# Modulation vectors of a two-block network: from matrix products on TensorE to dot products on VectorE, as a third stream of the plan

## The chip, the cores and the metric

One core of one Trainium2 chip runs the whole program. The metric is device time in microseconds (us), from three runs of the kernel before: 3962.25, 3965.93 (the median) and 3976.16. Names as in the profile: PE is TensorE (PEld its weight loads), DVE is VectorE, ACT is ScalarE, POOL is GpSimd, SP is SyncE, which only issues transfers.

## The reference, cut to what matters

A first block (two layers of a retention and state-space mixer and a feed-forward network) acts on `x`, 256 tokens of 1024 channels. A second block (two layers) mixes tokens and routes each token to 128 experts (PEER), for `x` and, in its first layer only, for a context `ctx` of 256 tokens. All is float32. Only the second block uses the modulation:

```python
def _modulation(cvec, w_mod, b_mod):
    m = jax.nn.silu(cvec) @ w_mod + b_mod          # [1,1024] @ [1024,6144]
    return jnp.split(m[:, None, :], 6, axis=-1)
def _modulate(x, g, shift, scale):
    return _rmsnorm(x, g) * (1 + scale) + shift
...
for l in range(2):
    m_x = _modulation(c, w_mod[l], b_mod[l])
    m_c = _modulation(c_ctx[None, :], w_mod[l], b_mod[l])
    h  = _modulate(x,   norm1_g[l], m_x[0], m_x[1])
    hc = _modulate(ctx, norm1_g[l], m_c[0], m_c[1])
    ...                                            # token mixing of hc and h
    x = x + m_x[2] * mix_x
    x = x + m_x[5] * _peer(_modulate(x, norm2_g[l], m_x[3], m_x[4]), ...)
    if l == 0:                                     # the same for ctx with m_c[2..5]
```

The context's mixing needs sixths 0 and 1 of `m_c` of layer 0 at first, and the others later. In layer 1 the context needs sixths 0 and 1 alone. The vectors for `x` aren't needed before the first block has ended.

## The kernel before

One Python class, `Plan`, writes one list of items in order (`put`), and each engine's program goes through the list and issues its part of each item. So the order of items is the order of instructions on every engine, and an engine that waits holds back all that stands behind it on that engine.

Two streams feed the list. Stream `a` is `x`: the first block, then the second. Stream `b` is the context: modulation, then its mixing (`mix_phase`), then its routing and experts (`peer_c`). `streams` (L228) takes the next piece of `b` whenever b's count of time has fallen behind `pace` times a's; each piece yields a count that is meant to be microseconds of its work. The paces are the table `PACES`, one for each stage. When the first block ends, what is left of `b` is put down at once. The counts of stream `a` are the same in both kernels, so they name a place in the program below: "count 257" is 257 counted microseconds into the first block. In the kernel before, modulation stands up to count 218, the context's mixing from there to 368, its routing to 477, and its 512 gathers with their products from 477 to 1699.

Modulation (L743): the weights of both layers come as 48 tiles of 1 MB (128 input channels by 2048 outputs), issued by POOL into a ring of seven slots (the semaphores wm0 to wm6), with up to four loaded ahead. For each, PE makes four products of 128x2 (both condition vectors) by 128x512 at four column positions of the array (L1905). After eight tiles DVE adds the bias, SP stores the rows to DRAM (`mod_store`), and PE and DVE turn them into columns (`mod_columns`, with four transposes at L1691).

The first block on PE is groups of 16 products of 128x128 by 128x256 at L1656, L1836 and L1843, on pairs of PSUM banks. A group's result is taken out by ACT or DVE before its bank is used again. The groups wait there on DVE: for the convolution (`conv_end`), for turning (L2200, L2308) and for the branch products (L2345). A head's routing on DVE (`rank_keys`, `rank_pairs`, `rank_index`) is a chain of small instructions. `peer_c` gathers rows on POOL (L2980), 0.5 MB each, and takes a dot product over 1024 channels with each (L2635, function `down`) or adds it (L2646, `up`), both on DVE. A weight tile of the first block goes over SP's queue into one of three slots.

A `Slot` is a piece of SBUF with a semaphore, a `Ring` a list of slots taken in turn; a load waits until the slot's last reader is done. `rstd` on POOL is L2967.

## Time and profile before

| | |
|---|---|
| median of three runs | 3965.93 us (3962.25 to 3976.16) |
| the profiled execution: its span, first to last instruction | 3961.4 us |
| lowest run, nearest to the profiled execution; outside its span | 3962.25 us; 0.85 us |
| PE busy | 3596.4 us, 91% |
| DVE busy | 2300.7 us, 58% |
| POOL busy | 1284.5 us, 32% |
| moved from HBM | 1201.64 MB read |

The profile doesn't give a time of its own for the profiled execution beside the span. The first and last instruction are the span's ends, and the lowest run is 0.85 us above it, so the span stands for that execution's time. In the tables below, busy time is the time in which an engine worked; a busy share near 100% on PE with little on the others means that PE is what the stage waits for. A matrix product in float32 leaves two records.

### The profile page before, as it was taken

The page shows a single profiled execution, that of the slowest core. Times are in us where ns is not written, and L with a number is a line of the kernel's source. Part 1 is how long each engine was busy: PE and PEld are TensorE (multiplying, and loading weights), DVE is VectorE, ACT ScalarE, POOL GpSimd, SP SyncE. Part 2 cuts the span into 40 slices and gives each one's busy share as a digit, 9 for nine tenths or more (in the row PEclk, how much of TensorE's full clock was granted, in tenths as well). Part 3 has the DMA queues.
Part 4 walks back from the last instruction along what each step waited for, and adds up shares of the span by engine and source line. Part 5 has one row for each costly group of instructions (what it writes and reads, how often), then busy time and mean ns, then how long its engine had stood idle before and what let it go on. Part 6 is the DMA issues. An engine that isn't in the chain of part 4 may idle for free. (4 is left out here: it accounts for less than half of the span.)

```text
span 3961.4 us, 41101 instructions
## 1 busy us (share of the span) xinstructions
PE 3596.4 (91%) x14600; PEld 2547.8 (64%) x14600; DVE 2300.7 (58%) x5460; ACT 664.2 (17%) x1814; POOL 1284.5 (32%) x1130
## 2 busy tenths in 40 slices
PE   8998999989999999999999989788779998877777
PEld 6667788878876888888847876333335786433333
DVE  3342013566877887765762147777763226777775
ACT  2232101110001330000002212111112211111111
POOL 1100000023445456774650013444341003444442
PEclk9999999999999999999999999899899999998999
DMA  8752345357998889998983259999996339999997
GB/s 331 291 202 89 128 149 191 128 207 291 345 354 343 292 296 412 406 400 343 414 353 132 102 221 411 398 414 407 411 419 274 108 126 375 405 419 419 420 419 327
DMA packets 206842, 1205.50 MB, mean 304 GB/s; under 512 B 23472, under 2 KB 24640, under 8 KB 95024
## 3 DMA queue, kind: packets, MB, share of 16 engines
q0 software_dynamic: 154976, 858.34, 54.0%
q1 hardware_dynamic: 51664, 344.55, 23.0%
q8 instruction: 118, 1.93, 0.2%
q14 instruction: 84, 0.69, 0.0%
HBM read 1201.64 MB, written 1.15 MB: 304 GB/s over the span
## 5 line engine op out<-in xcount | busy, mean ns | idle before, releaser
L1656 PE MATMUL bank<-big 128*128 128x256 f32 (+4 forms) x8888 | 1909.3, 374 | 47.3 <-DVE big L2435 13.8
L1656 PEld LDWEIGHTS bank<-big 128*128 128x128 f32 (+2 forms) x8888 | 1628.9, 190 | 338.3 <-issue 90.8
L2980 POOL DMA_INDIRECT big<-in_pboth,big x1024 | 1213.2, 1185 | 1301.0 <-PE bank L2134 703.7
L2134 PE MATMUL bank<-big 128*128 128x512 f32 x2048 | 990.6, 641 | 224.7 <-ACT big L2943 224.6
L2635 DVE CUSTOM_DVE_ANT_0 big<-big 128x1024 f32<-128x1024 f32 x768 | 926.1, 1223 | 338.6 <-DMA big<-in_pboth,big 333.2
L2134 PEld LDWEIGHTS bank<-big 128*128 128x128 f32 x2048 | 409.6, 204 | 785.8 <-issue 483.8
L2646 DVE SCALAR_TENSOR_TENSOR big<-big 128x1024 f32<-128x1024 f32 x254 | 326.1, 1284 | 75.7 <-DMA big<-in_pboth,big 55.3
L2967 POOL TENSOR_TENSOR big<-big 128x1 f32<-128x1 f32 (+1 forms) x49 | 42.4, 865 | 914.5 <-DVE big L2192 914.3
L2943 ACT ACTIVATE big<-big 128x128 f32<-128x128 f32 x512 | 165.4, 391 | 270.5 <-DVE big L2612 266.0
L2933 ACT ACTIVATE big<-big 128x4 f32<-128x4 f32 (+2 forms) x136 | 28.1, 207 | 730.9 <-DVE big L2608 725.6
L1836 PE MATMUL bank<-big 128*128 128x256 f32 x576 | 129.5, 378 | 0.0
L1691 PE MATMUL bank<-big 128*128 128x128 f32 x628 | 95.3, 284 | 32.8 <-ACT big L2721 17.2
L1836 PEld LDWEIGHTS bank<-big 128*128 128x128 f32 x576 | 108.7, 189 | 15.8
L1865 PE MATMUL bank<-big 128*128 128x512 f32 x256 | 110.6, 592 | 2.2 <-DVE big L2359 2.2
L1843 PE MATMUL bank<-big 128*128 128x256 f32 x448 | 103.0, 381 | 6.0 <-DVE big L2308 4.6
L1691 PEld LDWEIGHTS bank<-big 128*128 128x128 f32 x628 | 77.0, 150 | 47.7 <-issue 29.3
L2480 DVE TENSOR_REDUCE big<-bank 128x1 f32<-128x512 f32 (+1 forms) x48 | 28.9, 602 | 135.2 <-PE bank L2004 135.1
L2345 DVE SCALAR_TENSOR_TENSOR big<-big,bank 128x256 f32<-128x256 f32 x32 | 13.5, 422 | 154.9 <-PE bank L1843 154.8
L2991 POOL DMA_DIRECT2D big<-in_iota x1 | 0.6, 584 | 306.3 <-DVE big L2516 306.3
L2249 DVE SCALAR_TENSOR_TENSOR big<-bank,big 128x255 f32<-128x255 f32 (+1 forms) x144 | 62.7, 478 | 60.8 <-ACT big L2735 59.1
L1843 PEld LDWEIGHTS bank<-big 128*128 128x128 f32 x448 | 84.7, 190 | 19.3 <-DVE big L2308 5.1
L2268 DVE SCALAR_TENSOR_TENSOR big<-big,bank 128x512 f32<-128x512 f32 x32 | 22.0, 687 | 124.0 <-ACT big L2750 114.8
(218 smaller groups left out, 2279.7 us busy)
## 6 DMA issues: line engine op xcount, KB each, us to landing
big<-in_w SPq DMA_DIRECT2D x104, 1024.0 KB
big<-in_wmod POOLq DMA_DIRECT2D x48, 1024.0 KB, 8.9
big<-in_wgu SPq DMA_DIRECT2D x44, 1024.0 KB
big<-in_wzg SPq DMA_DIRECT2D x36, 1024.0 KB, 4.8
big<-in_wro SPq DMA_DIRECT2D x32, 1024.0 KB
big<-in_wpq SPq DMA_DIRECT2D x24, 1024.0 KB, 4.9
big<-in_wd SPq DMA_DIRECT2D x22, 1024.0 KB
big<-in_pboth,big POOLq DMA_INDIRECT x1024, 11.0
```

What stands on the lines that cost most here:

```text
L1656: last = pe.matmul(o, a, b, start=(i == 0), stop=(i == n - 1))
L1691: last = pe.transpose(o[:, i, :], b, ident)
L1836: pe.matmul(u.ap[:, 0:256], wk[:, k, :], YT[:, k, :], start=(k == 0), stop=False)
L1843: last = pe.matmul(u.ap[:, 0:256], wk[:, k, :], YT[:, k, :], start=False, stop=(k == 15))
L1865: last = pe.matmul(u.ap, act[:, 2 * i + k, tt * P:tt * P + P], wk[:, k, 512 * n:512 * n + 512], start=(i + k == 0), stop=False)
L2134: last = pe.matmul(u.ap, d.ap, row[:, 512 * i:512 * i + 512], start=(k == 0), stop=(k == 127))
L2249: i = v.scalar_tensor_tensor(c[:, m, s:256], o[:, m, 0:256 - s], conv["w"][m][:, 3 - s:4 - s], c[:, m, s:256], ALU.mult, ALU.add)
L2635: v.tensor_tensor_reduce(row, row, h, 1.0, 0.0, ALU.mult, ALU.add, out).then_inc(done[0], 1)
L2646: v.scalar_tensor_tensor(at, s.ap, by, at, ALU.mult, ALU.add).then_inc(done[0], 1)
L2943: s.activation(d.ap, p.ident, ACT.Copy, scale=by).then_inc(diag[0], 1)
L2967: g.tensor_tensor(r.sm[:, 8 + r.at:8 + r.at + r.n], r.sm[:, 4 + r.at:4 + r.at + r.n], r.sm[:, 12:13].to_broadcast([P, r.n]), ALU.pow).then ...
L2980: g.indirect_dma_start(out=s.ap, out_offset=None, in_=table, in_offset=bass.IndirectOffsetOnAxis(ap=index, axis=0)).then_inc(s.full[0], 16)
```

## The change

1. The modulation becomes a third stream `m`. It advances while its own count is below `MOD_PACE` = 0.6 times a's. The context calls it directly where it needs more.
2. Its work moves to DVE. The vector silu(c) lies as a row of 1024 on all 128 partitions. A block is 128 output channels by 1024 inputs (0.5 MB), and one dot product on DVE (`tensor_tensor_reduce`) gives one column. There are 160 blocks: for the context 48 of layer 0 and 16 of layer 1, then for `x` 48 of each layer. The weights are read once for each vector, 80 MB in place of 48.
3. The blocks' slots: one spare (wm0) from the start to the end of the context's mixing, two (wm1, wm2) in the memory of `MT` until the first layer's merging, and from there, in the memory of `fw`, one (wm3).
4. The context's mixing begins when sixths 0 and 1 are there. Before its routing the plan waits for its other sixths; after its routing, before its first gather, the plan puts down all blocks that are left.
5. The columns come straight out of the dot products. Rows for DRAM are made with one 128x48 transpose on PE, one copy on DVE and one store on SP (`mod_rows`), three times. The bias is loaded into the columns at the start.
6. `PACES` changes at three places: 0.79, 0.47 and 0.73 become 0.66, 0.41 and 0.66. One gather slot (`row_end`) is made of the vector's memory.

In the counts of stream `a`: the context's mixing stands from 30 to 183, its routing to 290, the last blocks end at 304, and the gathers stand from 304 to 1691.

```diff
 
-PACES = (0.8, 1.8, 1.5, 0.79, 0.47, 0.73, 4.0)
+PACES = (0.8, 1.8, 1.5, 0.66, 0.41, 0.66, 4.0)
+MOD_PACE = 0.6
+MOD_END = 1024
 A_SIZE = 27648
 BIG_N = 53208
 SIDE = 8300
...
+        self.mod_ring, self.mod = Ring([self.mod_spare]), self.modulation()
+        self.streams(self.x_stream(ar), self.context_stream(), self.mod, PACES[0])
...
+        live = {"a": a, "b": b, "m": m}
         while live:
             which = "b" if "b" in live and (tb <= ta * pace or "a" not in live) else "a"
+            if "m" in live and tm < ta * MOD_PACE:
+                which = "m"
             step = next(live[which], "over")
             if step == "over":
...
+                tm += step
...
+        self.tick("d_ctx", 16)
+        yield 16
+        while (0, 1, 1) not in self.sixths:
+            next(self.mod)
+            yield 2
         self.put("context_in")
         yield "pace", PACES[1]
+        ar.size -= 1024
         yield from self.mix_phase(self.pb, Ring(few), self.smallb, ar, 0, self.C, 1, False)
+        self.mod_moves([self.mod_spare], [])
+        while (0, 1, 5) not in self.sixths:
+            next(self.mod)
+            yield 2
...
+        mod_slots = [Slot(MT.rearrange("p a b -> p (a b)")[:, 1024 * i:1024 * i + 1024], self.sem(f"wm{i + 1}")) for i in range(2)]
+        mod_late = Slot(fw, self.sem("wm3"))
+        self.mod_ring.slots.extend(mod_slots)
...
                 yield "pace", PACES[4]
+                for _ in self.mod:
+                    pass
...
+            else:
+                mod_late.freed = cv.slots[cv.at % 2 - 1].freed
+                self.mod_moves(mod_slots, [mod_late])
+                put("mod_moved", ready=[w.freed for w in mod_slots])
...
+    def mod_moves(self, gone, new):
+        self.mod_ring = Ring([w for w in self.mod_ring.slots if w not in gone] + new)
+        while any(w.freed == "held" for w in gone):
+            next(self.mod)
...
-                for k in range(8):
-                    while srcs and len(coming) < 4:
-                        coming.append(self.load(wr, srcs.pop(0), 2048))
-                        put("mod_weights", w=coming[-1])
-                    w = coming.pop(0)
-                    done = tick("mod_part", 4)
-                    w.free(done)
-                    if k == 3 and late:
-                        part_end()
-                    put("mod", w=w, u=u, cc=cc, k=k, ready=(self.sem("mod_c_done"), 1) if l + part + k == 0 else None,
-                        done=done)
-                    yield 3
...
+        blocks = [(l, v, b) for v in (1, 0) for l in range(2) for b in range(16 if l and v else 48)]
+        left, coming, at, done = list(blocks), [], None, None
...
+        for l, v, b in blocks:
+            if v != at:
+                tmp, at = self.mod_room().take(), v
...
+                put("mod_c", dst=vector, tmp=tmp, src=t["crow"][v].to_broadcast([P, 1024]), before=done, loaded=tick("d_c2", 16),
+                    tanh=tick("mod_tanh"), done=ready)
+                tmp.free(ready)
+            while left and left[0][1] == v and self.mod_room():
+                l2, _, b2 = left.pop(0)
+                coming.append(self.load(self.mod_room(), t["wmod"][l2, b2], 1024))
+                put("mod_weights", w=coming[-1])
+            w, done = coming.pop(0), tick("mod_part")
+            w.free(done)
+            put("mod", w=w, vector=vector, to=sums[b // 8 % 2][:, b % 8:b % 8 + 1], done=done)
+            if b % 8 == 7:
...
+                self.cols_ok = tick("mod_columns")
...
+                put("mod_sixth", sums=sums[part % 2], ready=done, dst=self.mcols[:, j, 8 * part:8 * part + 8], gain=gain,
...
+                self.sixths.add((l, v, part))
+                if part == 5:
+                    s, u, self.mods_ok[l, v] = self.mod_room().take(), self.pb.take(), tick("d_mods", 16)
...
+                    put("mod_rows", src=self.mcols[:, j, :], u=u, ready=self.cols_ok, s=s, rows=s.ap[0:48, 0:P],
+                        dst=self.mods[l, v].rearrange("s (k p) -> (s k) p", p=P), done=self.mods_ok[l, v])
+                    s.free(self.mods_ok[l, v])
+            yield 1.25
...
+        while (l, vec) not in self.mods_ok:
+            next(self.mod)
+        put("load_row", dst=m2, src=self.mods[l, vec, 2:3, :].to_broadcast([P, 1024]), done=m2_ok,
+            before=[got["aT"], got["f_ok"], self.mods_ok[l, vec]])
...
         yield from route()
+        for _ in self.mod:
+            yield 2
...
-    def mod(w, u, cc, k, ready, done):
-        if ready:
-            pe.wait_ge(*ready)
-        if k == 0:
-            opened(u)
-        pe.wait_ge(*w.full)
-        for j in range(4):
-            pe.matmul(u.ap[32 * j:32 * j + 2, :], cc[:, k, :], w.dst[:, 512 * j:512 * j + 512], start=(k == 0),
-                             stop=(k == 7), tile_position=(0, 32 * j)).then_inc(done[0], 1)
...
+        pe.transpose(u.ap[0:48, 0:P], src, ident).then_inc(u.full[0], 1)
 
...
+        v.tensor_scalar(dst, dst, 0.5, None, ALU.mult).then_inc(done[0], 1)
+        v.wait_ge(*done)
+
+    def mod(w, vector, to, done):
+        v.wait_ge(*w.full)
+        v.tensor_tensor_reduce(w.dst, w.dst, vector, 1.0, 0.0, ALU.mult, ALU.add, to).then_inc(done[0], 1)
+
+    def mod_sixth(sums, ready, dst, gain, biased, done):
+        v.wait_ge(p.sem("d_bias"), 16)
+        v.wait_ge(*ready)
+        i = v.tensor_tensor(dst, dst, sums, ALU.add)
+        if gain:
+            i.then_inc(biased[0], 1)
...
+    def mod_rows(u, rows, dst, done, **_):
...
     def mod_load(gb, sc, sh, srcs, loaded, before):
         for ok in before:
@@ -3050,7 +3073,8 @@
         q.dma_start(cs.rearrange("p a b -> p (a b)"), t["cs"]).then_inc(done[0], 16)
```

DVE at the start of the program, before (L2377 and L2379 make silu(c), L2192 is the variance, L2200 takes the turned rows out of PSUM for the first product):

```order
L2407 MEMSET big 128x512
L2377 SCALAR_TENSOR_TENSOR big<-big 128x16 [waits mod_tanh,vector_step]
L2379 TENSOR_SCALAR big<-big 128x16 [waits vector_step]
L2192 TENSOR_SCALAR big<-big 128x1 [waits squares_done] x2
L2200 TENSOR_TENSOR big<-bank,big 128x4x128 [waits full4]
L2200 TENSOR_TENSOR big<-bank,big 128x4x128 [waits full5]
L2200 TENSOR_TENSOR big<-bank,big 128x4x128 [waits full4]
```

and now (L2403, L2405: silu(c) as rows; L2410: a block's dot product and, as its second row, the read of its sum; L2226 is L2200 of before):

```order
L2218 TENSOR_SCALAR big<-big 128x1 [waits squares_done]
L2403 SCALAR_TENSOR_TENSOR big<-big 128x1024 [waits mod_tanh]
L2405 TENSOR_SCALAR big<-big 128x1024 [waits vector_step]
L2410 ISA big<-big 128x1024 [waits wm1,mod_vector]
L2410 ISA big 128x1
L2410 ISA big<-big 128x1024 [waits wm2]
L2410 ISA big 128x1
L2410 ISA big<-big 128x1024 [waits wm0]
L2410 ISA big 128x1
L2226 TENSOR_TENSOR big<-bank,big 128x4x128 [waits full4]
L2226 TENSOR_TENSOR big<-bank,big 128x4x128 [waits full5]
L2410 ISA big<-big 128x1024 [waits wm1]
```

Three blocks now stand ahead of the first take-out and a fourth between the two halves.

PE around the small product for the time steps (128x32), before, where the modulation's first products stand (L1905), and below it now, where the context's first transposes and products stand (L1727 and L1692, bank pair 6 and 7):

```order
L1656 MATMUL bank<-big 128x256 x15
L1656 MATMUL bank<-big 128x32 [waits wa1,free5,free0]
L1656 MATMUL bank<-big 128x32 x15
L1905 MATMUL bank<-big 2x512 [waits wm0,mod_c_done]
L1905 MATMUL bank<-big 2x512 x3
L1905 MATMUL bank<-big 2x512 [waits wm1]
L1905 MATMUL bank<-big 2x512 x3
L1656 MATMUL bank<-big 128x256 [waits wa2,free1]
L1656 MATMUL bank<-big 128x256 x7
```

```order
L1692 MATMUL bank<-big 128x256 x7
L1727 MATMUL bank<-big 128x128 [waits rows_scaled]
L1727 MATMUL bank<-big 128x128 x7
L1692 MATMUL bank<-big 128x256 x8
L1727 MATMUL bank<-big 128x128 [waits rows_scaled_v,free6]
L1727 MATMUL bank<-big 128x128 x3
L1727 MATMUL bank<-big 128x128 [waits free7]
L1727 MATMUL bank<-big 128x128 x3
L1692 MATMUL bank<-big 128x128 [waits free7,wb0,free6]
L1692 MATMUL bank<-big 128x128 x15
L1692 MATMUL bank<-big 32x256 [waits free7]
```

The products of two rows are gone, and the context's projection stands inside and behind the fourth group.

DVE in the first layer's merging, around the take-outs of branch products 0 and 1, before (L2308 takes out turned rows, L2345 a branch product, L2480 to L2484 the context's attention):

```order
L2484 RECIPROCAL big<-big 128x1 [waits free6]
L2308 TENSOR_TENSOR big<-bank,big 128x4x128 [waits full5]
L2308 TENSOR_TENSOR big<-bank,big 128x4x128 [waits full4]
L2345 SCALAR_TENSOR_TENSOR big<-big,bank 128x256 [waits full0,free0]
L2480 TENSOR_REDUCE big<-bank 128x1 [waits full7,free6]
L2482 TENSOR_SCALAR big<-big 128x1 [waits vector_step]
L2484 RECIPROCAL big<-big 128x1 [waits free7]
L2345 SCALAR_TENSOR_TENSOR big<-big,bank 128x256 [waits full1,free0]
L2480 TENSOR_REDUCE big<-bank 128x1 [waits full6,free7]
L2482 TENSOR_SCALAR big<-big 128x1 [waits vector_step]
```

and now, from the take-out of product 1 on (L2371), at the end of the context's routing (L2613 to L2619 its gates):

```order
L2371 SCALAR_TENSOR_TENSOR big<-big,bank 128x256 [waits full1,free0]
L2410 ISA big<-big 128x1024 [waits wm3]
L2410 ISA big 128x1
L2613 TENSOR_REDUCE big<-big 128x8 [waits vector_step,gates_exp]
L2615 TENSOR_SCALAR big<-big 128x8 [waits vector_step]
L2617 RECIPROCAL big<-big 128x8 [waits vector_step]
L2619 TENSOR_TENSOR big<-big 128x128 [waits vector_step]
L2410 ISA big<-big 128x1024 [waits wm3,gates_done]
L2410 ISA big 128x1
L2410 ISA big<-big 128x1024 [waits wm3]
L2410 ISA big 128x1
L2410 ISA big<-big 128x1024 [waits wm3]
```

Behind these rows come eleven more blocks on slot wm3 before the next take-out. Every block from the merging on waits for `wm3`: 31 of them. On PE, behind the third branch product at this place, stands the transpose of `mod_rows`, which waits for the column sums of the last of these blocks (`mod_columns`).

## Rows read from the trace of the kernel before

**Rows 1.** The page: busy time of each engine, share of the span.
```profile
PE 3596.4 (91%) x14600; PEld 2547.8 (64%) x14600; DVE 2300.7 (58%) x5460; ACT 664.2 (17%) x1814; POOL 1284.5 (32%) x1130
```

**Rows 2.** Windows by stage: length, busy us of each engine, clock, DMA share, GB/s.
```profile
0.00:263.00 263.00, 245.91 (x1434) 177.39 (x1435) 107.01 (x257) 72.66 (x189) 28.39 (x56) 1.00 0.76 296
263.00:640.00 377.00, 348.61 (x1656) 292.87 (x1655) 59.30 (x143) 62.87 (x169) 3.90 (x6) 0.96 0.34 125
640.00:800.00 160.00, 155.52 (x746) 133.45 (x745) 78.77 (x255) 22.41 (x51) 5.59 (x9) 1.00 0.43 157
800.00:2081.00 1281.00, 1237.89 (x5534) 1007.00 (x5533) 930.75 (x1677) 153.23 (x367) 672.55 (x532) 0.99 0.89 345
2081.00:3961.00 1880.00, 1608.50 (x5237) 937.08 (x5235) 1124.90 (x3130) 353.05 (x1039) 574.12 (x528) 0.94 0.81 327
```

**Rows 3.** Groups on PE by form: count of records, busy us, mean ns.
```profile
L1656 PE MATMUL bank<-big 128*128 128x256 f32 x7984 | 1772.4, 380 | 27.5 <-issue 6.6 <-DVE big L2268 5.5 <-DVE big L2200 3.6
...
L1691 PE MATMUL bank<-big 128*128 128x128 f32 x628 | 95.3, 284 | 32.8 <-ACT big L2721 17.2 <-ACT big L2769 8.5 <-DVE big L2337 4.3
L1905 PE MATMUL bank<-big 128*2 128x512 f32 x384 | 48.8, 592 | 0.0
```

**Rows 4.** Groups on DVE by form: count, busy us, mean ns.
```profile
L2635 DVE CUSTOM_DVE_ANT_0 big<-big 128x1024 f32<-128x1024 f32 x768 | 926.1, 1223 | 338.6 <-DMA big<-in_pboth,big 333.2 <-issue 3.0
...
L2635 DVE DVE_READ_ACCUMULATOR2_ANT big<- 128x1 f32 x768 | 63.3, 82 | 0.0
...
L2402 DVE TENSOR_TENSOR big<-big 128x1024 f32<-128x1024 f32 x2 | 2.5, 1226 | 0.1
```

**Rows 5.** Timeline of the start: start us, us, engine, line.
```profile
14.37 1.04 ACT L2704 ACTIVATE big<-big 128x1024 f32<-128x1024 f32 x1
...
17.70 3.96 POOL L2973 DMA_DIRECT2D big<-in_wmod  x7
...
19.34 1.29 DVE L2200 TENSOR_TENSOR big<-bank,big 128x512 f32<-128x512 f32 x2 [2.23 <-PE bank L1691]
...
22.14 31.49 PE L1656 MATMUL bank<-big 128*128 128x256 f32 x160 [0.79 <-DVE big L2200]
...
30.43 2.69 DVE L2249 SCALAR_TENSOR_TENSOR big<-bank,big 128x255 f32<-128x255 f32 x6 [8.35 <-ACT big L2735]
33.15 0.63 ACT L2743 ACTIVATE big<-big 128x512 f32<-128x512 f32 x1 [2.75 <-DVE big L2249]
33.81 0.69 DVE L2261 SCALAR_TENSOR_TENSOR big<-big 128x512 f32<-128x512 f32 x1 [0.70 <-ACT big L2743]
```

**Rows 6.** DMA issues: queue, count, KB, us from issue to landing.
```profile
big<-in_wmod POOLq DMA_DIRECT2D x48, 1024.0 KB, 8.9
...
big<-in_wout SPq DMA_DIRECT2D x12, 1024.0 KB, 4.8
...
big<-in_wukv SPq DMA_DIRECT2D x4, 512.0 KB, 3.3
```

**Rows 7.** The modulation's weight loads: issue times in ns, and time to landing.
```profile
L2973 POOL DMA_DIRECT2D big<-in_wmod x48: 527/537/760, 17.7 to 233.7; - x48
...
DMA to landing us min/median/max: 5.2/8.9/21.6
```

**Rows 8.** Timeline of DVE over most of one head's routing, first and last.
```profile
689.77 0.30 DVE L2529 MAX8 big<-big 128x8 f32<-128x128 f32 x1
...
691.62 0.42 DVE L2548 TENSOR_TENSOR big<-big 128x256 f32<-128x256 f32 x1
...
698.40 1.41 DVE L2337 SCALAR_TENSOR_TENSOR big<-bank,big 128x512 f32<-128x512 f32 x2
```

**Rows 9.** Waits over the span: who waited for whom, us, times, longest.
```profile
DVE big L2345 <- PE bank L1843: 154.8, 31, 32.8
```

**Rows 10.** Windows of 20 us in the context's mixing; columns as in Rows 2.
```profile
260.00:280.00 20.00, 13.85 (x82) 10.82 (x75) 9.91 (x26) 12.18 (x31) 1.82 (x3) 0.83 0.36 138
...
540.00:560.00 20.00, 20.00 (x94) 17.47 (x93) 3.88 (x6) 1.68 (x4) 0.00 (x0) 1.00 0.46 163
```

**Rows 11.** The context's gathers on POOL: issue times in ns, first and last start.
```profile
L2980 POOL DMA_INDIRECT big<-in_pboth,big x512: 932/1112/2055, 841.0 to 2049.9; - x171
```

196 lines of the change are left out of this document (82 added, 114 removed).

## The prediction

> **What bounds the kernel now.** I read the page's busy times first: PE is busy 91% of the span, DVE 58% [rows 1]. Then the windows by stage [rows 2]. The change acts in the first block, 0 to 2081 us. PE is busy there 245.9 + 348.6 + 155.5 + 1237.9 = 1988 of 2081 us, so nearly every microsecond taken from PE's work there is one less, and nearly every new idle one is one more. DVE has room on average: 107 + 59 + 79 + 931 = 1176 us busy. But the reader is to see in the order of DVE's instructions that it is one queue. The third view is the waits: DVE waits 154.8 us for the branch products [rows 9], so in the first layer's merging PE sets the pace and DVE stands ready. The stages behind 2081 us are not touched.
>
> **What goes from PE.** L1905 is busy 48.8 us in 384 records [rows 3], all of it in a stage where PE is nearly full. The 24 transposes that made columns are 48 records of 95.3/628 = 0.152 us each: 7.3 us. Three transposes of 48 rows come back, under 1 us. Sum: -56 us, with ends at -49 (transposes hidden in gaps) and -68 (12 us more of PE's gaps around them). I take -56.
>
> **What comes to DVE.** A block is the operation of `down`: 1.223 us, and 0.082 for the read of its sum [rows 4], so 1.305 us. 160 of them are 209 us, which on average fit in the 905 us in which DVE is idle. Each vector costs a product and a scaling besides, about 2 us, twice. So the price is not the work. It is what stands behind a block in DVE's queue while the block waits for its weights.
>
> **The round trip of a slot.** A block frees its slot, POOL issues the next load (0.53 us [rows 7]), it lands, and DVE goes on. No row has a 0.5 MB load by POOL alone. From below: the same size by SP lands in 3.3 us [rows 6]. From above: the 1 MB loads of POOL, which overlap each other, have a median of 8.9 and a least of 5.2 us [rows 7]. The 1 MB loads by SP take 4.8 [rows 6], 1.5 more than the half; 5.2 less 1.5 is 3.7, and some 0.5 us for the release and POOL's own step brings it to 4.2 us, which I take, as the nearest row is the least of POOL's. I call this e, with ends 3.3 and 8.9.
>
> [...]
>
> **Start of the program, +15.** PE's first group starts at 22.1 us, right behind the take-outs of L2200 [rows 5]. Now three blocks stand ahead of these and a fourth between them. The first load is issued when POOL has done the reciprocal roots, at about 17.7 as before [rows 5]; it lands near 21, the third near 22.5, the last take-out ends near 28. That is 6 us. In the four convolution groups DVE has 2.69 + 0.69 us of its own for each of PE's 7 us [rows 5], and now 3.4 blocks of 1.305: 7.8 us in 7, plus about 2 us whenever four blocks stand in a row for three slots (e less two blocks). PE loses some 9 us more until the context gives it other work. Ends: 5 (landings early enough) and 25.
>
> **The context's mixing, +15.** Here PE's work for both streams is the same as before, moved 190 counts earlier. DVE was busy 59 of 377 us [rows 2]; 76 blocks bring 99 us, and the first block's own share of DVE is larger at this place (107 in 263 us [rows 2]). There is room, but every take-out can find a block ahead of it, and PE was idle 28 us here by such chains already. Two places stop SP's queue as well: the store of `mod_rows` waits for DVE, and the second vector's load waits for DVE's last block of the first; the weight tile behind each is issued only then and lands 4.8 us later [rows 6], in place of two groups ahead. I take 5 us for each of them and 5 for collisions; ends 0 and 35.
>
> **The context's routing, +35.** From count 183 to 257 PE has about 105 us of work: rows 2 show 155.5 us for the same eight queries beside 109 counts of `x`; the new place to 304 has 12 counts more, so 167, less the 62 of the next part. DVE has 35 blocks (46 us), five heads of routing at 10.6 us (6.7 from the pairs to the last cast, and 2 x 1.9 for the keys [rows 8]: 53 us), about 10 for the context's rows, about 27 for `x` (0.36 of 75, the share of rows 2's first window), and since the spare slot is gone, seven times a third block waits e less one block, 2.9 us: 20. That is 156 us against 105. PE can stay ahead by its banks for a group or two, so I take 35 of the 51; ends 0 and 51.
>
> **The single slot, +121.** From the merging on all 31 blocks wait for wm3. No load can be under way while a block is computed. On DVE: 31 x 1.305 = 40.5, three heads 32, take-outs and gates 6, and the exposed round trips: 22 blocks follow another block directly (e each), four more follow something short of e (together about 3e - 2). With e = 4.2 that is 25 x 4.2 - 2 = 103. Sum 181, and with the waits for the gates' exponent 183 us. PE's work at this place, counted in its order: 128 products of 128x256 at 2 x 1772.4/7984 = 0.444 us and 16 of 128x128 at 0.30 [rows 3], 62 us. Can PE run ahead and hide it? It can't: the first branch product's end needs the turned rows, which DVE takes out behind the first 13 blocks, and then PE has 20 us of work until the transpose of `mod_rows`, which waits for the last block's sum, with 18 blocks before it. So PE waits 183 - 62 = +121 us. With e = 3.3 it is +99, with e = 8.9 +239.
>
> **Afterwards, -8.** The gathers get 1387 counts in place of 1222, so DVE and the DMA engines (0.89 full in rows 2) are less dense; PE is idle 43 us there, and I take 8 of them back; ends 0 and -20. The context still ends ahead of the first block (1691 of 1722), so there is no tail. A granted clock of 0.83, mostly the full 2.4 GHz and in part 1.2, shows where PE was idle a third of 20 us [rows 10]; PE's work behind the new waits may run so, but DVE is what ends there, so I add nothing.
>
> **Sum.** -56 + 15 + 15 + 35 + 121 - 8 = +122 us. 3961.4 + 122 = 4083 against the profiled execution's own span; the median of the runs shown lies 4.5 above it, half of which I grant: 4085 us.
>
> **Rivals.**
> 1. *The stalls don't reach PE.* Loads land as fast as DVE asks and PE's banks cover the rest: -56 - 8 and about 15 at the start and at SP's queue: 3915 us, faster than before. For it: DVE waits for PE 154.8 us at L2345 alone [rows 9], so it often has time. Against it: the transpose of `mod_rows` ties PE to DVE's last block. It decides if e is under about 1 us. Chance 0.14.
> 2. *Only the last run of blocks counts.* DVE gets far enough ahead of PE before; then 14 blocks in a row cost 14 x 5.5 - 20 = 57 in place of 121, and the routing stage nothing: 3961 - 56 + 30 + 57 - 8 = 3984 us. Chance 0.15. Against it: DVE's heads need PE's queries first.
> 3. *The round trip is as long as the median of 8.9 us.* +239 in place of +121: about 4200 us. For it: POOL's loads by rows 7. Against it: these had up to four others under way, these here have none. Chance 0.07.
> 4. *The context comes late* and leaves a tail behind the first block, since its paces are smaller: 2 to 4% of the gathers' 1280 us, 4120 us. Chance 0.03; its counts end 31 ahead.
>
> The Trainium skill ("SBUF — State Buffer", the trap in which DVE blocks DMA) says that GpSimd can't write a load's descriptors while DVE holds the shared port. By that rule a block would lengthen the next block's load, up to one block each, 1.3 x 25 = 33 us, and speak for rival 3. The 48 issues of rows 7 took 527 to 760 ns beside a DVE busy 0.4 of the time, so the trace shows none of it; and with one slot DVE stands still while the load is made.
>
> **How the numbers follow.** The forecast has 0.58, the rivals 0.14, 0.15, 0.07 and 0.03, and 0.03 is left for a time near the old one. Its own range, from e and the ends of the other terms, is 4030 to 4150. The range for all reaches down to rival 2: 3960 to 4160 holds 0.80, leaving out rival 1 and most of rival 3. Within 0.3% is 3954 to 3978, about what a measurement of this kernel can't tell from no change: 0.05, from the rest and the low edge of rival 2. Faster 0.15, slower 0.80.
>
> **What would show it.** Right: on DVE, idle time before the block's line put down to the DMA of the modulation's weights, some 100 us of it within a stretch of 180 us in which PE is busy a third; the transpose of 48 rows on PE with a wait of tens of us; PE's first group near 28 us; the first gather near 757 us in place of 841 [rows 11]: at count 304 the program has 477 - 304 = 173 us less behind it than the 800 us of count 477, 56 us less of products and 186 us more of stalls. POOL's load there every 5.5 us. Wrong: PE above 90% in every window before 700 us (rival 1), or a landing under 2 us, or the wait sitting in gathers after 700 us.

## The result, and the profile after

The changed kernel takes 4191.30 us (median of four runs, 4188.10 to 4191.73) against 3964.61 beside it: ratio 1.0572, 95% interval 1.0553 to 1.0590. The forecast was 4085 with a range from 3960 to 4160. The sign was right, but +122 us should have been +227, and the time lies outside the range.

The page's busy times after, columns as in [rows 1]:

```profile
PE 3568.5 (85%) x14195; PEld 2557.3 (61%) x14195; DVE 2477.4 (59%) x5772; ACT 664.1 (16%) x1815; POOL 1337.8 (32%) x1242
```

PE lost 28 us of work and gained 253 us of idle time. Windows by stage, as in [rows 2]: to the end of the context's mixing, its routing, the single slot up to the first gather, the rest of the first block, the second block.

```profile
0.00:532.00 532.00, 412.44 (x1945) 347.69 (x1945) 230.83 (x498) 109.21 (x285) 56.82 (x106) 0.89 0.55 199
532.00:715.00 183.00, 133.07 (x666) 114.68 (x667) 122.30 (x332) 37.82 (x102) 23.54 (x43) 0.88 0.55 196
715.00:898.00 183.00, 43.86 (x202) 37.58 (x200) 73.80 (x201) 3.96 (x8) 18.50 (x33) 0.64 0.33 103
898.00:2305.00 1407.00, 1369.17 (x6147) 1121.11 (x6147) 925.26 (x1613) 159.77 (x380) 651.61 (x533) 0.99 0.86 329
2305.00:4186.70 1881.70, 1609.92 (x5240) 936.20 (x5239) 1125.23 (x3131) 353.30 (x1041) 587.31 (x528) 0.94 0.81 327
```

The second block is as before. In the third row PE is busy a quarter of the time and DVE under half of it: both wait. Who waits there, from the groups of DVE and the waits of DVE and of PE (engine, line, for whom, us, times, longest); L2410 is a block, L1937 the transpose of `mod_rows`, L1879 the branch product's end, L2334 the take-out of turned rows:

```profile
L2410 DVE CUSTOM_DVE_ANT_0 big<-big 128x1024 f32<-128x1024 f32 x160 | 192.9, 1222 | 171.5 <-DMA big<-in_wmod 170.8
```
```profile
PE bank L1937 <- DVE big L2415: 104.6, 3, 73.1
PE bank L1879 <- DVE big L2334: 66.0, 1, 66.0
```

73.1 + 66.0 = 139.1 us is all of PE's idle time in the single-slot stage. And this is one turn of the slot on DVE and POOL (timeline: start, us, engine, line, idle time before it):

```profile
722.44 1.23 DVE L2410 CUSTOM_DVE_ANT_0 big<-big 128x1024 f32<-128x1024 f32 x1
723.59 0.08 DVE L2410 DVE_READ_ACCUMULATOR2_ANT big<- 128x1 f32 x1
723.97 0.53 POOL L2996 DMA_DIRECT2D big<-in_wmod  x1 [5.79 <-DVE big L2410]
...
727.76 1.23 DVE L2410 CUSTOM_DVE_ANT_0 big<-big 128x1024 f32<-128x1024 f32 x1 [4.08 <-DMA big<-in_wmod]
728.91 0.08 DVE L2410 DVE_READ_ACCUMULATOR2_ANT big<- 128x1 f32 x1
729.29 0.53 POOL L2996 DMA_DIRECT2D big<-in_wmod  x1 [4.79 <-DVE big L2410]
```

The block ends, POOL issues the next load 0.3 us later, DVE stands 4.08 us until it has landed. The forecast had taken 4.2. The 32 loads of this stage land 3.6 to 4.6 us after the start of their issue, 3.8 in the median, and DVE waits for 27 of them, 105.5 us in all.

### The profile page after: what moved, and what is told of

It is laid out like the page before. It is cut to its first block and busy times, and to the rows that moved or that the text cites. A ratio compares the mean times of both kernels' runs of the same rounds, so it can differ in the third digit from the quotient of the medians.

```text
span 4186.7 us, 40723 instructions
## 1 busy us (share of the span) xinstructions
PE 3568.5 (85%) x14195; PEld 2557.3 (61%) x14195; DVE 2477.4 (59%) x5772; ACT 664.1 (16%) x1815; POOL 1337.8 (32%) x1242
## 5 line engine op out<-in xcount | busy, mean ns | idle before, releaser
L1692 PE MATMUL bank<-big 128*128 128x256 f32 (+6 forms) x8888 | 1919.3, 376 | 79.6 <-DVE big L2456 21.5
L1692 PEld LDWEIGHTS bank<-big 128*128 128x128 f32 (+2 forms) x8888 | 1640.4, 191 | 352.1 <-issue 89.7
L2160 PE MATMUL bank<-big 128*128 128x512 f32 x2048 | 994.5, 643 | 222.3 <-ACT big L2966 221.2
L2656 DVE CUSTOM_DVE_ANT_0 big<-big 128x1024 f32<-128x1024 f32 x768 | 925.1, 1223 | 319.3 <-DMA big<-in_pboth,big 317.4
L2160 PEld LDWEIGHTS bank<-big 128*128 128x128 f32 x2048 | 411.3, 205 | 785.8 <-issue 490.1
L2996 POOL DMA_DIRECT2D big<-in_wmod x160 | 85.2, 533 | 700.5 <-DVE big L2410 675.7
L2990 POOL TENSOR_TENSOR big<-big 128x1 f32<-128x1 f32 (+1 forms) x49 | 48.4, 988 | 799.9 <-DVE big L2218 799.9
L2410 DVE CUSTOM_DVE_ANT_0 big<-big 128x1024 f32<-128x1024 f32 x160 | 192.9, 1222 | 171.5 <-DMA big<-in_wmod 170.8
L1879 PE MATMUL bank<-big 128*128 128x256 f32 x448 | 105.4, 388 | 69.3 <-DVE big L2334 66.0
L1727 PE MATMUL bank<-big 128*128 128x128 f32 x604 | 92.2, 284 | 70.0 <-ACT big L2742 25.0
L1872 PE MATMUL bank<-big 128*128 128x256 f32 x576 | 132.6, 385 | 10.4 <-DMA big<-in_wro 10.4
L1879 PEld LDWEIGHTS bank<-big 128*128 128x128 f32 x448 | 86.7, 194 | 83.5 <-DVE big L2334 66.2
L1872 PEld LDWEIGHTS bank<-big 128*128 128x128 f32 x576 | 110.8, 193 | 27.5 <-issue 11.0
L1727 PEld LDWEIGHTS bank<-big 128*128 128x128 f32 x604 | 73.9, 150 | 83.9 <-ACT big L2742 16.7
L1937 PE MATMUL bank<-big 128*48 128x128 f32 x3 | 1.1, 381 | 104.6 <-DVE big L2415 104.6
L2725 ACT ACTIVATE big<-big 128x1024 f32<-128x1024 f32 x26 | 27.4, 1055 | 375.2 <-DVE big L2391 141.2
```

Of the source, the lines that this page charges most:

```text
L1692: last = pe.matmul(o, a, b, start=(i == 0), stop=(i == n - 1))
L1727: last = pe.transpose(o[:, i, :], b, ident)
L1872: pe.matmul(u.ap[:, 0:256], wk[:, k, :], YT[:, k, :], start=(k == 0), stop=False)
L1879: last = pe.matmul(u.ap[:, 0:256], wk[:, k, :], YT[:, k, :], start=False, stop=(k == 15))
L2160: last = pe.matmul(u.ap, d.ap, row[:, 512 * i:512 * i + 512], start=(k == 0), stop=(k == 127))
L2410: v.tensor_tensor_reduce(w.dst, w.dst, vector, 1.0, 0.0, ALU.mult, ALU.add, to).then_inc(done[0], 1)
```

## What the experiments measured

The runs fall into two kinds. Some take one cost out of the changed kernel while its order stays (e1, e2, e3, e13); the others move the work (e4, e5, e6, e7, e9, e12) or measure a piece of it at another place (e8, e10, e11, e14, e15). The kernel before took 3963 to 3965 us beside all of them. Runs without all loads or products (e1, e2, e3, e8, e10, e11, e13, e14) leave out values of the modulation and serve only to measure time; e4 to e7, e9, e12 and e15 compute all of it. e2, e3, e4, e5, e6, e10 and e11 have two executions each, which lie 0.5 to 7 us apart. Theory at the start: round trips of a slot are the price. First rival: the work itself on DVE. Second rival: the order, since the context's chains now stand beside the program's first groups.

**e1_bare_order.** Neither waits for weights nor work of blocks.

```diff
-                coming.append(self.load(self.mod_room(), t["wmod"][l2, b2], 1024))
-                put("mod_weights", w=coming[-1])
+                w = self.load(self.mod_room(), t["wmod"][l2, b2], 1024)
+                coming.append(w)
+                if w.slot.count > 16:
+                    w.slot.count -= 16
+                    w.full = None
+                else:
+                    put("mod_weights", w=w)
...
-        v.wait_ge(*w.full)
-        v.tensor_tensor_reduce(w.dst, w.dst, vector, 1.0, 0.0, ALU.mult, ALU.add, to).then_inc(done[0], 1)
+        if w.full:
+            v.wait_ge(*w.full)
+        elif w.before:
+            v.wait_ge(*w.before)
+        v.tensor_tensor_reduce(w.dst[:, 0:8], w.dst[:, 0:8], vector[:, 0:8], 1.0, 0.0, ALU.mult, ALU.add, to).then_inc(done[0], 1)
```

> The changed kernel's order of items, but only the first block on each of the four slots is loaded, and each block's product goes over 8 channels in place of 1024, so blocks cost DVE next to nothing and wait for nothing (the modulation's values are left out). Theory (the blocks' waits and work are the whole loss): 3961 - 56 - 8, and 20 for the start and SP's queue, about 3920 us, and PE idle under 30 us from 60 to 300 us. Rival (the context's mixing, moved to the front, stalls PE by its own chains, blocks or not): PE stays idle 60 to 80 us between 60 and 300 us, and the time is about 3980 us.

Measured: 3973.8 us (3970.39 to 3977.08). With the blocks' cost gone, the kernel is still no faster than before (ratio 1.0020, 1.0006 to 1.0034), though PE has some 50 us less to do. So the theory falls. The rival has the time (3980), but not all of its mechanism: PE idles 48 us from 60 to 300 us, against 10.5 before, and not 60 to 80; and e13 below shows that 30 us of the time come from SP's queue and not from the context's chains.

**e2_no_loads** keeps the products over 1024 channels and drops the loads as in e1; **e3_late_no_loads** drops only those of slot wm3.

```diff
+                if w.ap.shape[1] == 1024 and w.slot is self.mod_late and w.slot.count > 16:
```

> The changed kernel, but only the first block on each slot is loaded; all 160 products over 1024 channels stay (on other data, so the modulation's values are left out). Theory (the round trips are the price, the work of 209 us on DVE is hidden): within 30 us above e1_bare_order. Rival (DVE's work itself is the price, since it stands in front of take-outs): 90 us or more above e1_bare_order, near 4050 us. What the changed kernel has above this run is the price of all waits for weights.

> The changed kernel, but of the 31 blocks on the single slot wm3 only the first is loaded; their products stay (on other data). Theory (25 exposed round trips of 4.1 us on the single slot): 4191 - 103 = about 4088 us, and PE's idle time in the stretch before the first gather falls from 139 to about 36 us. Rival (what holds PE there is the order, 13 and 18 blocks' work in a row in front of take-outs and the transpose): no more than 40 us less, 4150 us.

Measured: e2 4048.8 us, e3 4086.5. So DVE's work costs 75.0 us above e1, between the two expectations (the blocks keep DVE busy for 194 us; the 209 of the forecast adds up a product of 1.22 us and a read of 0.08 that overlap); the round trips with two or three slots cost 37.7 (e3 less e2); those of the single slot 104.8 (the changed kernel less e3), where 103 were forecast. Both runs take the loads' bytes away together with the waits; on the single slot DVE's waits in the trace, 105.5 us, are the whole of it. The same windows in e3:

```profile
532.00:715.00 183.00, 130.90 (x659) 112.65 (x657) 122.81 (x328) 36.97 (x101) 23.87 (x43) 0.88 0.55 199
715.00:801.00 86.00, 47.11 (x217) 40.38 (x217) 76.92 (x213) 5.35 (x12) 2.75 (x4) 0.81 0.14 49
```

The first row is close to that of the changed kernel; the second stage takes 86 in place of 183 us, PE's idle time falls from 139 to 39 (theory: 36), and DVE is now busy 77 of 86.

**e13_sp_free** (run later, after the waits of e1 had been read). It is e1, with this edit.

```diff
-    def mod_c(dst, src, before, loaded, **_):
-        if before:
-            q.wait_ge(*before)
-        q.dma_start(dst, src).then_inc(loaded[0], 16)
-
-    def mod_rows(u, rows, dst, done, **_):
-        q.wait_ge(*u.free)
-        q.dma_start(dst, rows).then_inc(done[0], 16)
...
+    def mod_c(dst, src, before, loaded, **_):
+        if before:
+            g.wait_ge(*before)
+        g.dma_start(dst, src).then_inc(loaded[0], 16)
...
+    def mod_rows(u, rows, dst, done, **_):
+        g.wait_ge(*u.free)
+        g.dma_start(dst, rows).then_inc(done[0], 16)
```

> e1_bare_order (the changed kernel's order, four loads, products over 8 channels), but the stores of mod_rows and the loads of the condition vector are issued by POOL and no longer by SP (as there, the modulation's values are left out). Theory (SP's queue stands up to 59.9 us for them, so that weight tiles of the first block come late: PE waits 13.7 us for in_w and 10.2 us for in_wro): 3974 - 24 = 3950 us, and both waits gone. Rival (PE would wait there anyway, for DVE): 3968 us or more.

Measured: 3943.7 us (3940.66 to 3945.78), 30 less than e1, and 0.9948 (0.9932 to 0.9964) of the kernel before. What SP waited for up to 640 us in e1 (L3044 is the first block's weight loads, L3067 the load of the condition vector, L3071 the stores of `mod_rows`):

```profile
SPq L3044 <- PE bank L1697: 435.8, 39, 31.7
SPq L3071 <- DVE big L2435: 93.0, 2, 49.1
SPq L3067 <- DVE big L2418: 59.9, 1, 59.9
```

and in e13:

```profile
SPq L3053 <- PE bank L1697: 592.3, 48, 53.4
```

SP came to these three instructions up to 60 us before DVE did, and the weight tiles behind them were issued only then. PE's waits in e1 for `in_w` (13.7 us), `in_wro` (10.6) and `in_wpq` (5.8) are gone in e13, and 21 of the 30 us are gained from 540 to 700 us (PE busy 145.9 in place of 124.8 us). The theory expected 24 and got 30. In e13 POOL stands up to 89.2 us for the same stores; there it has almost no loads of blocks behind them. The same move in the changed kernel, where POOL has 160, was not run.

**e4_spread and e5_spread_early_load.** The 31 late blocks are spread over the gathers (`MOD_LATE` is 0.08), which have 8 slots in place of 9.

```diff
-            if "m" in live and tm < ta * MOD_PACE:
+            if "m" in live and tm < min(ta, 257) * MOD_PACE + max(ta - 257, 0) * MOD_LATE:
...
-        for _ in self.mod:
-            yield 2
```

> The changed kernel, but the plan doesn't put down all blocks that are left ahead of the first gather: from count 257 on a block comes every 15 counts (MOD_LATE 0.08), and the gathers have 8 slots in place of 9, since the vector's memory is in use. Theory (the run of blocks on one slot is the price, and single blocks between gathers cost nothing, DVE being ahead there): 4191 - 133 + a few us for the missing gather slot, 4065 us. Rival (the price moves along, each single block holding up DVE for its landing of 4 us between the gathers' products): 4150 us or more.

Measured: 4180.5 us. The theory fell: 11 us gained in place of 126. DVE's waits for the weights grew from 171 to 240 us, the longest from 6.7 to 12.8. One of them (POOL L2999 is a gather, L2992 the block's load, DVE L2652 a gather's product, L2406 the block):

```profile
1196.14 0.59 POOL L2992 DMA_DIRECT2D big<-in_wmod  x1
...
1196.24 0.39 ACT L2826 ACTIVATE big<-bank 128x256 f32<-128x256 f32 x1 [1.15 <-PE bank L1688]
1197.04 0.97 POOL L2999 DMA_INDIRECT big<-in_pboth,big  x1 [0.30 <-issue]
1205.65 1.23 DVE L2406 CUSTOM_DVE_ANT_0 big<-big 128x1024 f32<-128x1024 f32 x1 [9.51 <-DMA big<-in_wmod]
```

The load stood in the plan directly in front of its block, and POOL issued it behind eight gathers of the last 17 us. It landed some 9.5 us later, and DVE, an engine with one queue, did nothing until then. Behind the block stood a take-out, which ACT waited for 14.5 us, and the products that free the gathers' slots: POOL waited 10.3 us for the next one. PE, which had groups left, waited 1.1 us at this place; from 800 to 1400 us it is idle 108 us (26 before). e5 puts the load half way between two blocks (`ahead` issues what the free slots can take):

```diff
-            yield 1.25
+            if len(left) < 32:
+                yield 0.6
+                ahead(v)
+                yield 0.65
+            else:
+                yield 1.25
```

> e4_spread, but each late block's load is put down half way after the block before it, and no longer directly in front of its own block. Theory (in e4_spread a load stood directly in front of its block and behind several gathers in the DMA queues, so that DVE stood 9.5 to 12.8 us for each): the waits of DVE for the modulation's weights behind the first gather fall from 170 to under 20 us, 4180 - 110 = about 4070 us. Rival (POOL, which waits with the load until DVE has done the block before, now issues the gathers late): DVE waits longer for gathers instead, 4150 us or more.

Measured: 4088.7 us, 92 less. DVE's waits for weights behind the first gather fell from 169.8 to 52.2 us, not to under 20. The place of the load is shown as the main cause; its new place was still short, since the loads from 850 us on land 3.7 to 13.7 us after their issue, 6.8 in the median.

**e6_context_late and e7_late_and_ahead.**

```diff
-        yield 16
+        yield 174
...
-PACES = (0.8, 1.8, 1.5, 0.66, 0.41, 0.66, 4.0)
+PACES = (0.8, 1.8, 1.5, 0.79, 0.47, 0.73, 4.0)
```

> The changed kernel, but the context's mixing begins at count 218 as in the kernel before, with that kernel's PACES; the blocks come from count 0 on at their pace of 0.6. Theory (a third of the loss is that the context's chains stand beside the first groups with few of x's groups to fill PE, +65 in e1_bare_order): 65 us less for that, and since the spare slot now lives past the merging, the late blocks have two slots and cost some 25 in place of 133 us: about 4020 us. Rival (the order costs nothing by its place, DVE's blocks cost the same wherever the context stands): 4120 us or more.

> e6_context_late with two things more: a slot is loaded again right behind the block that frees it in the plan, and not only ahead of the next block; and from count 257 on the blocks come at half the pace (MOD_LATE 0.3, one every 4.2 counts). Theory (waits for weights go if loads are asked for early and blocks stand apart): DVE's waits for the modulation's weights under 40 us, PE's idle time before the first gather near 80 us, about 3950 us, at or under the kernel before. Rival (the work of 209 us on DVE itself costs 75 us, as e2_no_loads had it against e1_bare_order, wherever it stands): 3990 us or more.

Measured: 4055.5 and 4044.5 us (ratio of e7 1.0199, 1.0181 to 1.0218). e6 gained 136 where 171 were expected. It changes two things, the context's place and, by the slot that lives longer, the late blocks' round trips (DVE's waits for weights fall from 171 to 104 us), and no run splits the 136. e7 added 11 in place of 70, and DVE's waits for weights are 69 us and not under 40, so its theory failed. PE, clock, DMA share and GB/s from 60 to 300 us, first e6, then e7:

```profile
60.00:300.00 240.00, 168.23 (x838) 0.83 0.73 257
```
```profile
60.00:300.00 240.00, 174.16 (x863) 0.84 0.74 263
```

PE idles 72 and 66 us here though the context's mixing is away. So in this stretch it is enough for a loss that blocks come at pace 0.6 (one per 2.1 counts) in front of the take-outs that x's own groups need. DVE waits 48 and 45 us for blocks' weights here, so these runs have the dense work and the waits together.

**e9_even, e10_even_no_loads, e11_even_bare.** On e6, the blocks are spread evenly:

```diff
-MOD_PACE = 0.6
+MOD_PACE = 0.27
+MOD_LATE = 0.27
```

> The changed kernel with the context at count 218 and the old PACES (as e6_context_late), and the blocks spread evenly, one every 4.6 counts from the start to about count 740 (MOD_PACE 0.27), each load put down half way between two blocks, nothing drained ahead of the gathers, 8 gather slots. Theory (what costs is blocks that stand close together in front of PE's take-outs and wait for weights; spread evenly, DVE's work hides): PE's idle time from 60 to 300 us falls from 66 us in e7_late_and_ahead to about 35, DVE's waits for the modulation's weights under 30 us, 3975 us. Rival (a block costs PE 0.36 us for each of its own, 75 of 209 us, wherever it stands, and the gathers' stage with its busy DVE gives nothing for free): 4020 us or more.

> e9_even, but only the first block on each slot is loaded (the modulation's values are left out); the products over 1024 channels stay. e9_even less this is the price of the 80 MB and the waits for them: under the theory about 10 us, under a rival in which the loads' bytes slow the gathers down, 30 us or more.

> e10_even_no_loads with products over 8 channels in place of 1024 (values left out): neither loads nor work on DVE. Theory (PE's 56 us come off, three quarters of them in time, as e8_before_thin had it for the products): 3965 - 42 = about 3923 us, and e10_even_no_loads stands about 30 us above it. Rival (the work on DVE costs 75 us also when spread): 75 us above it.

Measured: 4165.5, 3994.1 and 3941.8 us. PE from 60 to 300 us and from 800 to 1400 us, in e9 and in e10:

```profile
60.00:300.00 240.00, 221.21 (x1193) 0.95 0.59 208
800.00:1400.00 600.00, 378.54 (x1515) 0.82 0.68 244
```
```profile
60.00:300.00 240.00, 221.24 (x1190) 0.95 0.30 105
800.00:1400.00 600.00, 521.60 (x2263) 0.94 0.79 289
```

Two things at once. Up to 800 us the even pace does what was hoped: PE idles 19 us in the first stretch (72 in e6), with or without loads, and DVE waits 0.3 us for weights there. Behind the first gather it fails: the blocks have one slot (wm3) at 4.6 counts each, and DVE waits 184.7 us for their loads, up to 11.0 for one. So e9 was wrong by 190 us, nearly all by its late part, a case that neither of its expectations had. The loads and the waits for them (e9 less e10) cost 171 us where the theory had about 10 and the rival 30 or more; DVE's waits are large enough for it, and whether the 80 MB also slow the gathers is not separated. The work alone (e10 less e11) costs 52 us in place of 75, between its two. e11 itself came at 3941.8 and not at 3923. It stands within 2 us of e13, which has the context early and SP's queue free: so over the whole program the early place of the context, with bare blocks, shows no price of its own. What PE loses there in the first 300 us, it loses less of from 800 to 1400 us (idle 14 us in e13, 43 in e11). e11 and e13 differ in other things too (a gather slot, SP's two kinds of stops), so this is a reading and not a test.

**e12_two_slots** gives the blocks a second slot in the gathers' stage (the gathers keep 7) and loads right behind the freeing block.

```diff
+MOD_PACES = ((0, 218, 0.27), (218, 360, 0.42), (360, 477, 0.22), (477, 4000, 0.16))
...
+        more = Slot(ar.get(1024), self.sem("wm4"))
+        more.freed = gates_ok[0, 0]
+        self.mod_ring.slots.append(more)
```

> The changed kernel with the context at count 218 and the old PACES; blocks at paces 0.27 to count 218, 0.42 to 360, 0.22 to 477 and 0.16 behind it (128 of 160 by count 530, the last at 781); each slot is loaded again right behind its block; in the gathers' stage a second slot (wm4) for blocks, taken from the gathers, which keep 7. Theory (e9_even stalled because one slot's turn in the gathers' stage, 6 to 11 us of landing, is longer than the blocks' spacing of 4.6 counts; two slots with 7 counts spacing give each load 14 counts): DVE's waits for the modulation's weights behind the first gather under 20 us, and the time is that of e10_even_no_loads plus a little, 3994 + 15 = about 4010 us. Rival (the 32 blocks' bytes and work in the gathers' stage, whose DMA share is 0.9, cost in themselves): 4040 us or more.

Measured: 4036.1 us (ratio 1.0186, 1.0169 to 1.0203). The first half of the theory holds: DVE waits 6.3 us for weights behind 850 us. The time is 26 above the theory's and near the rival's. PE idles 78 us from 800 to 1400 us (26 before). In e10, which has the work but no loads there, it is 78 also, and in e11, which has neither, 43: so 35 of the 52 us are the work, and 17 come with the new order and its gather slots. And it idles 44 us from 300 to 800 us (27 in e10); I put that down to the pace of 0.42, which no run tests alone. It has the lowest time of the arrangements with all 160 blocks on DVE.

**e8_before_thin.** What are the products worth on PE?

```diff
+            n = 512 if k in (0, 7) else 8
-            pe.matmul(u.ap[32 * j:32 * j + 2, :], cc[:, k, :], w.dst[:, 512 * j:512 * j + 512], start=(k == 0),
+            pe.matmul(u.ap[32 * j:32 * j + 2, 0:n], cc[:, k, :], w.dst[:, 512 * j:512 * j + n], start=(k == 0),
```

> The kernel before, with six of each eight modulation products narrowed from 512 to 8 columns (part of the modulation's sums is left out); loads, waits and order stay. It measures what the products' time on PE is worth. Theory (each microsecond of them is on the path, -48.8 for all): 36.6 us of them go, 144 narrow ones come with perhaps 10 us: 3935 to 3940 us. Rival (PE waits there for weights anyway, or other gaps open): 3955 us or more.

Measured: ratio 0.9949 (0.9932 to 0.9966), 20 us less (13 to 27). The groups of e8 at this line:

```profile
L1906 PE MATMUL bank<-big 128*2 128x512 f32 x96 | 12.3, 591 | 0.0
L1906 PE MATMUL bank<-big 128*2 128x8 f32 x288 | 7.5, 170 | 1.5 <-DMA big<-in_wmod 1.5
```

PE's work fell by 48.8 - 12.3 - 7.5 = 29.0 us, and 20 of them came off the time: about 0.7 of a microsecond each (0.45 to 0.9). I take it that part of these products filled gaps; no run shows which.

**e14_third_on_dve and e15_hybrid.** How much may go to DVE? In the kernel before, 16 of 48 tiles go to DVE, with all else as it was (their sums are left out).

```diff
+                    on_v = k in {2: (2, 5), 5: (4, 6)}.get(3 * l + part, (1, 3, 5))
+                    if on_v:
+                        done_v = tick("mod_part_v", 2)
+                        w.free(done_v)
+                        put("mod_v", w=w, done=done_v)
```

> The kernel before, with 16 of the 48 weight tiles of the modulation taken off PE: in place of their four products DVE takes two dot products over 1024 on each (the sums of these tiles are left out of the vectors). The 1 MB loads, their seven slots, the context's place and all else stay. It asks what moving only as much as costs no byte more would bring: PE 16 x 4 x 0.254 = -16.3 us, three quarters of it in time by e8_before_thin, -12; DVE +42 us in a stretch where it is busy 107 of 263 us. Theory (with four tiles under way DVE never waits for weights, and its work costs a quarter at most, +10): 3963 us, no change that can be told. Rival 1 (the work hides wholly): 3952 us. Rival 2 (0.36 us of PE for each on DVE, as in e2_no_loads against e1_bare_order): 3968 us or more.

Measured: ratio 0.9983 (0.9974 to 0.9992), 7 us less (3 to 10): between theory and rival 1, and rival 2 is out. DVE waits for no weights there. e15 does it completely, for the sixths 2 to 5 of layer 1 that x alone needs. There a 1 MB tile serves one vector anyway, so no byte is added:

```diff
+        srcs = [t["wmod"][l, part, k] for l, part in ((0, 0), (0, 1), (0, 2), (1, 0)) for k in range(8)]
+        for i in range(16):
+            srcs.insert(3 * i + 1, t["wmodv"][i])
...
+    def mod_v(w, vector, to, done):
+        v.wait_ge(*w.full)
+        for i in range(2):
+            a = w.dst[:, 1024 * i:1024 * i + 1024]
+            v.tensor_tensor_reduce(a, a, vector, 1.0, 0.0, ALU.mult, ALU.add, to[:, i:i + 1]).then_inc(done[0], 1)
...
+    t["wmodv"] = i["w_mod_2"][1, :, 2048:].T.reshape(16, 2, 128, 1024).transpose(0, 2, 1, 3).reshape(16, 128, 2048)
```

> The kernel before, complete, but the last four sixths of layer 1 for x alone (which the context doesn't need) are computed on DVE: 32 dot products on 16 tiles of 1 MB, one tile behind each two of PE's 32, from the same ring (now six slots, four tiles ahead). The bytes stay the same. Against e14_third_on_dve come the vector's row (two operations of 1.2 us), one transpose and one store, and two stores and eight transposes go. Theory (e14_third_on_dve was 7 us faster; the additions are hidden or worth 3 us at most): 3957 us, faster than both kernels, ratio 0.998. Rival (the vector's row and tanh stand in front of the first take-outs, as the blocks did in the changed kernel, and take it back): 3964 us or more.

Measured: 3949.2 us (3946.26 to 3954.52), ratio 0.9967 (0.9955 to 0.9979). It beats both kernels: 13 us (8 to 18) less than before. Its 32 blocks on DVE:

```profile
L2411 DVE CUSTOM_DVE_ANT_0 big<-big 128x1024 f32<-128x1024 f32 x32 | 37.9, 1221 | 0.1
```

0.1 us of idle time before them, where the changed kernel has 171.5. Why it gains 6 us more than e14 is not settled. It also has eight transposes and eight small stores less and one transpose, one store and the vector's row more, and the two intervals (3 to 10, 8 to 18) overlap.

## Why the prediction was wrong in size

First by stages, from the windows of the profiled executions (PE's idle time now less that of before, and what the prediction had):

| part | forecast | measured |
|---|---|---|
| start and the context's mixing (0 to 532 us; before 0 to 540) | +15 +15 | 119.6 - 43.9 = +76 |
| the context's routing (532 to 715; 540 to 640) | +35 | 49.9 - 1.6 = +48 |
| single slot (715 to 898; 640 to 841) | +121 | 139.1 - 5.8 = +133 |
| afterwards, to the first block's end | -8 | 37.8 - 41.8 = -4 |
| PE's busy time up to there | -56 | 1958.5 - 1988.0 = -30 |
| second block | 0 | +1 |
| sum | +122 | +224 |

The first row can be parted. Up to 60 us PE idles 22.4 us now and 12.8 before, +10; from 60 to 300 us 82.0 and 10.5, +71; behind that it is 5 us less than before. So the start came about as forecast (+15), and the whole excess is in the context's mixing, +66 in place of +15.

Then by causes, from the runs. They were taken off one on top of the other, and another order could part the sum in another way:

| cause | us |
|---|---|
| products gone, the context earlier, SP's three waits gone (e13 less before) | -21 |
| SP's queue stopped by the vector's load and two stores (e1 less e13) | +30 |
| DVE's work (e2 less e1) | +75 |
| round trips with two or three slots (e3 less e2) | +38 |
| round trips of the single slot (the changed kernel less e3) | +105 |
| sum | +227 |

**The round trip and the single slot: right.** e was forecast at 4.2 us; the loads landed in

```profile
DMA to landing us min/median/max: 3.5/4.1/10.6
```

and the 25 exposed trips, 103 us, cost 104.8. The Trainium skill ("DMA: Bandwidth & Descriptors", the anatomy of one DMA) gives about 2.0 us fixed and the bytes at 436 GB/s for a load issued by GpSimd, an estimate of 3.2 us for 0.5 MB. It lies below the least of the 160 landings, 3.5 us, which are counted from the start of the issue. The Trainium skill ("SBUF — State Buffer", the trap in which DVE blocks DMA) states its rule for DVE operations in a mode that takes two ports, so the prediction's 33 us stretch it to operations that it doesn't name. The trace shows nothing of it for these dot products: POOL's 160 issues take 527 to 760 ns, as before, beside a denser DVE.

The signs came as named: the first branch product's end waits 66.0 us, the transpose of 48 rows 73.1, POOL issues every 5.3 us (5.5 in the forecast). Rivals 1, 2 and 3 are out: PE does wait, the runs of blocks before the last one count too, and e isn't 8.9. Rival 4 is out as well: the context's last gather starts at 2243.5 us, before the first block ends.

**The context's mixing, +15, is the step that failed: it measured +66.** I counted DVE's room (59 of 377 us busy), gave collisions between blocks and take-outs 5 us and SP's two stops 5 each, and gave nothing for the context's new place. PE's busy time, clock, DMA share and GB/s from 60 to 300 us, in the kernel before, e13, e1, e2 and the changed kernel:

```profile
60.00:300.00 240.00, 229.54 (x1366) 0.98 0.67 263
60.00:300.00 240.00, 196.26 (x988) 0.93 0.22 79
60.00:300.00 240.00, 192.14 (x939) 0.89 0.19 70
60.00:300.00 240.00, 169.01 (x785) 0.82 0.16 61
60.00:300.00 240.00, 158.05 (x751) 0.80 0.46 162
```

PE is idle 10.5, 43.7, 47.9, 71.0 and 82.0 us. Taken in this order, the context's early place makes 33 us, SP's queue 4, the blocks' work 23 and the waits for weights 11. The forecast had 5 us in place of the first and the third together. Over the whole program the parts weigh otherwise:
- *SP's stops cost 30 us over the whole, not 10* (measured with bare blocks, e1 less e13). In the context's mixing the forecast was near: up to 532 us PE waits 16.4 us for tiles of SP's queue, 4.5 before. What it lacked is that SP runs far ahead: it stood 70.8 us for the vector's load and 120.1 for two stores in the changed kernel, and tiles far behind came late too, for another 16.3 us of waits after 532 us.
- *The work isn't free where DVE has room on average.* I wrote that the price is not the work. e2 less e1 says 75 us for 160 blocks. As I read it, a take-out that finds a block ahead of it is up to 1.3 us late, and at one block per 2.1 counts many do; no run counts them. In e14 the same kind of work, in its old surroundings and never waiting, costs little.
- *Round trips with two or three slots cost 38 us.* The forecast had 20 in the context's routing, 2 at the start and none in the mixing.
- *The chains of the context lengthen with each block in them.* PE's second longest wait here is one such step: the context's low-rank rows (variance on DVE, root on POOL L2990, scaling on ACT L2860, transpose on PE), with a block at the head of DVE's queue that waits for its weights:

```profile
118.09 1.23 DVE L2410 CUSTOM_DVE_ANT_0 big<-big 128x1024 f32<-128x1024 f32 x1 [6.67 <-DMA big<-in_wmod]
119.24 0.08 DVE L2410 DVE_READ_ACCUMULATOR2_ANT big<- 128x1 f32 x1
119.24 0.17 DVE L2218 TENSOR_SCALAR big<-big 128x2 f32<-128x2 f32 x1
...
119.49 0.71 POOL L2990 TENSOR_TENSOR big<-big 128x2 f32<-128x2 f32 x1 [7.52 <-DVE big L2218]
...
120.23 0.84 ACT L2860 ACTIVATE big<-bank,big 128x256 f32<-128x256 f32 x2 [11.41 <-POOL big L2990]
...
121.13 0.48 PE L1727 MATMUL bank<-big 128*128 128x128 f32 x1 [13.07 <-ACT big L2860]
```

PE had stood since 108.1 us: DVE did three blocks (3.4 us), waited 6.7 us for the fourth's weights and did the fourth, and the chain over POOL and ACT took another 1.9 us.

The two main parts, the context's early place and the dense blocks with their waits, don't add up, so the 33 and the 23 and 11 us above hold only for that order: with the context late and the dense pace, PE still idles 72 us from 60 to 300 us (e6); with the early context and bare blocks 44 (e13); with neither 19 (e9). Of the 71 us that are lost here, the dense blocks alone make 61 and the early place alone 33.

**What goes from PE, -56: too much.** The forecast counted two records for each of 24 transposes, 7.3 us; the traces have 14600 - 14195 = 405 records less, which is 384 of the products and 24 - 3 of transposes. So a transpose leaves one record, and these 24 were about 3 us (L1691 95.3 us in 628 records, L1727 92.2 in 604). With that some 51 us of work went, and PE's busy time fell by 28 over the span. I had written that a lower clock behind the new waits adds nothing. The granted clock is 0.80 from 60 to 300 us and 0.64 in the stage of the single slot, so there it lay part of the time at the lower of its two levels (1.2 of 2.4 GHz) after PE had stood idle, and records there are longer: 443 ns for the 32 of L1879 behind the wait of 66.0 us, where the whole group has 388 now and 381 before. The main group's mean is 382 ns now and was 380 ([rows 3]), which is 9 us over its 7984 records:

```profile
L1692 PE MATMUL bank<-big 128*128 128x256 f32 x7984 | 1781.5, 382 | 46.3 <-DMA big<-in_w 15.6 <-DMA big<-in_wpq 5.9 <-issue 5.5
```

L1872 and L1879 have another 5.5 us, the second block's products of 128x512 (L2160) 3.9, and small groups the rest of the 23 us that came back. That the clock makes these microseconds is my reading; no run holds it fixed. And e8 says that only about 0.7 of each microsecond taken there shows in the time.

**The context's routing, +35 for +48, and afterwards, -8 for -4: in their ranges.** The first hardly changes when wm3's loads are gone (52.1 us idle in e3, 49.9 in the changed kernel); 23.5 us of it is the second transpose of `mod_rows`, which waits for the last sums of x's layer 0.

**Two of the signs.** PE's first group came at 31.3 us, not near 28. The first gather came at 898.2, not near 757; that sign was worked out wrongly as well. It counts from 800 us, the end of a window, where [rows 11] have the gather at 841.0. From there the forecast's sum gives 798, and the 100 us that are left are the error of the sum up to there (46 + 13 + 12 + 26 in the table, 97).
